# Sixteen more tokens taken out of the dense expert products and served by gathered rows, with GpSimd and ScalarE doing their arithmetic

## The reference

```python
q = (xf @ wq).reshape(t, PEER_HEADS, PEER_QDIM)
s1, s2 = q_first_half @ keys1.T, q_second_half @ keys2.T
v1, i1 = lax.top_k(s1, PEER_TOPK); v2, i2 = lax.top_k(s2, PEER_TOPK)
...                                   # the best 16 of the 16 x 16 sums of each head
expert = ...                          # (t, 128) numbers of experts
gate = jax.nn.softmax(top_s, axis=-1).reshape(t, -1)
z = jnp.einsum('cd,ced->ce', xc, u[ec])
act = jax.nn.gelu(z, approximate=False) * gc
out = jnp.einsum('ce,ced->cd', act, v[ec])
```

## Time and profile before

| | us |
|---|---|
| median of three runs | 3151.75 |
| lowest of them | 3145.31 |
| the profiled execution | 3146.41 |
| its span, first to last instruction | 3144.4 |
| TensorE busy | 3106.8 (99%) |
| VectorE busy | 2407.6 (77%) |
| ScalarE busy | 1743.9 (55%) |
| GpSimd busy | 308.2 (10%) |
| the eight PEER blocks, U0 to V3 | 1764.6 to 3130 of the span |

### The profile page before, as it was taken

How to read it: one execution, slowest core, us unless ns; L and a number is a source line. 1 busy time by engine, 2 the same in 40 slices (tenths; PEclk the granted TensorE clock), 3 DMA queues, 4 the chain that set the end, 5 groups by cost and what they waited for, 6 DMA issues and landing times.

```text
span 3144.4 us, 62060 instructions
## 1 busy us (share of the span) xinstructions
PE 3106.8 (99%) x24748; PEld 3003.6 (96%) x24748; DVE 2407.6 (77%) x3908; ACT 1743.9 (55%) x2400; POOL 308.2 (10%) x303
## 2 busy tenths in 40 slices
PE   9999999999999999999999999999999999999998
PEld 9999999999999999999999988999999999999997
DVE  8767777755556776666668999988799789988887
ACT  6444545777776655555655455554555545554454
POOL 2000000000000000000000022331133112210110
PEclk9999999999999999999999999999999999999999
DMA  5444435444444545555455555678867787665785
GB/s 203 147 160 148 169 115 211 161 169 163 160 164 171 185 168 182 176 180 177 164 188 180 185 199 202 245 264 287 297 236 251 274 287 249 244 214 188 259 291 194
DMA packets 117821, 637.37 MB, mean 203 GB/s; under 512 B 11633, under 2 KB 32497, under 8 KB 50417
## 3 DMA queue, kind: packets, MB, share of 16 engines
q1 hardware_dynamic: 98496, 565.49, 50.7%
q0 software_dynamic: 18864, 68.43, 6.7%
q10 hardware_dynamic: 288, 1.05, 0.1%
HBM read 632.57 MB, written 2.36 MB: 202 GB/s over the span
## 4 chain that ended last, share of the span: by engine, by line
PE 86%; DVE 8%; DVEq 2%; ACT 2%; DMA 1%; issue 1%; ACTq 0%; SPq 0%
PE bank L670 14%; PE bank L672 14%; PE bank L671 14%; PE bank L1153 11%; PE bank L1206 9%; PE bank L1154 5%; PE bank L1207 5%; DVE wl L1856 3%; PE bank L1196 2%; PE bank L1198 2%; PE bank L1197 2%; PE bank L1117 1%; PE bank L824 1%; PE bank L1156 1%; ACT wh L1344 1%
## 5 line engine op out<-in xcount | busy, mean ns | idle before, releaser
L1856 DVE TENSOR_TENSOR wl<-raw,wh 128x1024 fp32r<-128x1024 f32 x1052 | 1267.1, 1238 | 349.9 <-ACT wh L1344 341.1
L1344 ACT ACTIVATE wh<-raw 128x1024 fp32r<-128x1024 f32 x1052 | 1052.7, 1050 | 394.3 <-DMA raw<-w_in_a 128.6
L671 PE MATMUL bank<-hhl,wh 128*128 128x256 f32 x3568 | 989.1, 277 | 0.0
L670 PE MATMUL bank<-hhl,wh 128*128 128x256 f32 x3440 | 966.9, 281 | 1.0 <-DVE hhl L1904 1.0
L672 PE MATMUL bank<-hhl,wl 128*128 128x256 f32 x3440 | 953.4, 277 | 0.0
L671 PEld LDWEIGHTS bank<-hhl,wh 128*128 128x128 f32 x3568 | 673.4, 189 | 1.9 <-issue 1.7
L670 PEld LDWEIGHTS bank<-hhl,wh 128*128 128x128 f32 x3440 | 647.9, 188 | 5.1 <-issue 2.4
L672 PEld LDWEIGHTS bank<-hhl,wl 128*128 128x128 f32 x3440 | 647.2, 188 | 0.0
L1153 PE MATMUL bank<-hhl,wh 128*128 128x448 f32 x1920 | 625.0, 382 | 6.8 <-DVE wl L1856 6.7
L1154 PE MATMUL bank<-hhl,wl 128*128 128x224 f32 x2048 | 522.4, 265 | 0.0
L1206 PE MATMUL bank<-ahl,wh 128*128 128x448 f32 x1488 | 472.1, 374 | 2.4 <-DVE ahl L2570 2.1
(11 more groups left out here) (461 smaller groups left out, 4405.2 us busy)
## 6 DMA issues: line engine op xcount, KB each, us to landing
raw<-peer_u SPq DMA_DIRECT2D x128, 1024.0 KB
raw<-peer_v SPq DMA_DIRECT2D x128, 1024.0 KB
raw<-w_in_c SPq DMA_DIRECT2D x64, 1024.0 KB
raw<-w_in_a SPq DMA_DIRECT2D x63, 1024.0 KB
raw<-w_kv SPq DMA_DIRECT2D x32, 1024.0 KB
raw<-w_in_b SPq DMA_DIRECT2D x32, 1024.0 KB
raw<-w_out_a SPq DMA_DIRECT2D x16, 1024.0 KB
raw<-w_out_b SPq DMA_DIRECT2D x16, 1024.0 KB
```

Source lines behind the costliest of these rows:

```text
L670: eng.matmul(out, h_[:, k, :], high[:, k, :], start=(k == 0), stop=False)
L671: eng.matmul(out, h_[:, k, :], low[:, k, :], start=False, stop=False)
L1344: eng.activation(high_half(c, half), raw_half(c, half), ACT.Copy).then_inc(hi_ready, 1)
L1856: eng.tensor_tensor(low_half_out(c, half), raw_half(c, half), high_half(c, half).bitcast(F32), ALU.subtract).then_inc(lo_ready, 1)
```

## The change

48 of the 256 tokens are now outside the dense products, so `DENSE` is 208: the wide matmuls have 416 columns, the narrow ones and those of V2 have 208, and there are 26 gate turns. The 32 tokens of before keep their path; three of `ROW_TURNS` are rewritten for 26 gate turns, with as many steps in each block as before.

The 16 new tokens (`MORE`) are spread as 16 tokens x 8 groups, which makes 16 steps of each of the 4 kinds, 64 in all. Each has an indirect DMA of 0.5 MB (`fetch_more`) into one buffer, `rows_more`. `MORE_AT` gives them turns: 20 in V0, 21 in V1, 13 in V2, 10 in V3.

- Products with `u` (steps 0 to 31, in V0 and in turns 0 to 14 of V1): GpSimd waits for the landing, multiplies the row by the tokens into `more_scaled`, and issues the next fetch; ScalarE's turn waits for GpSimd and sums `more_scaled` with a copy that accumulates.
- Sums with `v` (steps 32 to 63): ScalarE's turn waits for the landing and scales the row by its activation; GpSimd adds it to `x_more` and fetches the next. In V2 ScalarE scales in place and GpSimd fetches after its addition; else the fetch comes before it.
- ScalarE's part (`weigh_more`) stands at the end of its turn, after `high_part`.
- SP gets 16 small DMAs ahead of the loads of U1 (keys and gates of the new rows) and 8 ahead of those of V0 (the tokens), VectorE a wait for the first of them, GpSimd 8 DMAs behind step 15.
- TensorE gets 8 small matmuls in each of the two `row_sums`, behind a wait for the last sum.
- Several small tiles move and share memory, and some semaphores of an earlier stage are merged; the order of that stage's work is as it was.

```diff
 LAST = P // GROUPS
-DENSE = T - LAST
+MORE = 16
+MORE_GROUPS = P // MORE
+ROWED = LAST + MORE
+DENSE = T - ROWED
 TURNS = DENSE // TG
 ROWS = SLOTS_PER_TOKEN // GROUPS
+MORE_ROWS = SLOTS_PER_TOKEN // MORE_GROUPS
+ALL_ROWS = ROWS + MORE_ROWS
 ROW_TURNS = {
-    "U1": [n for n in range(3, BJ) if n % 2 == 1 or n >= TURNS],
+    "U1": [n for n in range(5, BJ) if n % 2 == 1 or n >= TURNS],
     "V0": [n for n in range(BJ) if n % 4 != 3 and n != 20 or n == 23],
-    "U2": [n for n in range(BJ) if n % 2 == 1 or n >= TURNS - 2],
+    "U2": [n for n in range(BJ) if n % 2 == 1 or n >= TURNS],
     "V1": [0, 1, 2, 4] + [n for n in range(9, BJ) if n % 4 != 3],
-    "U3": [n for n in range(TURNS + 1) if n % 2 == 1 or n >= TURNS],
+    "U3": [n for n in range(TURNS + 2) if n % 2 == 1 or n >= TURNS],
     "V2": [20, 22, 24, 26, 28, 29, 30, 31],
     "V3": [n for n in range(27) if n % 8 != 7],
 }
@@ -70,6 +75,21 @@
 for _k, _v in ROW_TURNS.items():
     for _n in _v:
         ROW_AT[_k, _n] = len(ROW_AT)
+assert len(ROW_AT) == 4 * ROWS
+MORE_TURNS = {
+    "V0": [n for n in range(BJ) if n % 8 in (0, 2, 3, 5, 6)],
+    "V1": [n for n in range(16) if n % 4 != 3] + [n for n in range(20, 30) if n != 24],
+    "V2": [n for n in range(13) if n % 2 == 0] + [n for n in range(20, BJ) if n % 2 == 0],
+    "V3": [n for n in range(23) if n % 5 in (0, 2)],
+}
+MORE_AT = {}
+for _k, _v in MORE_TURNS.items():
+    for _n in _v:
+        MORE_AT[_k, _n] = len(MORE_AT)
+assert len(MORE_AT) == 4 * MORE_ROWS
+MORE_GELU_AT = 17
+MORE_GATED_AT = 17
+MORE_IN_PLACE = range(MORE_AT["V2", 0], MORE_AT["V3", 0])
...
+                if (name, b) == ("U", 1):
+                    eng.wait_ge(sQ["x_out"], 16)
+                    eng.wait_ge(sQ["slots_step"], 1)
+                    eng.sem_inc(sp_passed, 1)
+                    for q in range(MORE_GROUPS):
+                        slots = slice(q * MORE_ROWS, (q + 1) * MORE_ROWS)
+                        eng.dma_start(row_keys[q * MORE:(q + 1) * MORE, :, ROWS:ALL_ROWS],
+                                      place[P - ROWED:P - LAST, NT - 1, :, slots]).then_inc(sQ["keys_in"], 16)
+                        eng.dma_start(row_gate[q * MORE:(q + 1) * MORE, ROWS:ALL_ROWS],
+                                      tops[P - ROWED:P - LAST, NT - 1].rearrange("p h k -> p (h k)")[:, slots]).then_inc(sQ["keys_in"], 16)
+                if (name, b) == ("V", 0):
+                    eng.wait_ge(sQ["slots_step"], 4)
+                    for q in range(MORE_GROUPS):
+                        eng.dma_start(x_more[q * MORE:(q + 1) * MORE, :], x_rows[0:MORE, 0:D // 2]).then_inc(sQ["more_x_in"], 16)
                 block_of(name, peer_u if name == "U" else peer_v, b)
...
+            def fetch_more(g):
+
+                kind, r = g // MORE_ROWS, g % MORE_ROWS
+                eng.indirect_dma_start(out=rows_more[:, :], out_offset=None, in_=peer_u_rows if kind < 2 else v_rows,
+                                       in_offset=bass.IndirectOffsetOnAxis(ap=left[kind // 2][:, kind % 2, ROWS + r:ROWS + r + 1], axis=0)).then_inc(more_in, 16)
+
+            def more_dot(g):
+
+                kind, r = g // MORE_ROWS, g % MORE_ROWS
+                eng.wait_ge(more_in, 16 * (g + 1))
+                if g > 0:
+                    eng.wait_ge(sQ["more_by_scalar"], g)
+                if r == 0 and kind == 0:
+                    eng.wait_ge(sQ["more_x_in"], 16 * MORE_GROUPS)
+                if r == 0 and kind == 1:
+                    eng.wait_ge(sQ["x_out"], 16 + 16 * MORE_GROUPS)
+                eng.tensor_tensor(more_scaled[:, :], rows_more[:, :], x_more[:, :], ALU.mult)
+                eng.drain().then_inc(sQ["more_by_gpsimd"], 1)
+                if kind == 0 and r == MORE_ROWS - 1:
+                    for q in range(MORE_GROUPS):
+                        eng.dma_start(x_more[q * MORE:(q + 1) * MORE, :], x_rows[0:MORE, D // 2:D]).then_inc(sQ["x_out"], 16)
+                fetch_more(g + 1)
+
+            def more_gates():
+
+                eng.wait_ge(sQ["more_by_scalar"], 2 * MORE_ROWS)
+                eng.tensor_tensor(row_dot[:, 0, ROWS:ALL_ROWS], row_dot[:, 0, ROWS:ALL_ROWS], row_dot[:, 1, ROWS:ALL_ROWS],
+                                  ALU.add).then_inc(sQ["more_step"], 1)
+                eng.wait_ge(sQ["more_step"], 2)
+                eng.tensor_tensor(row_act[:, ROWS:ALL_ROWS], row_act[:, ROWS:ALL_ROWS], row_gate[:, ROWS:ALL_ROWS],
+                                  ALU.mult).then_inc(sQ["more_step"], 1)
+
+            def more_sum(g):
+
+                r = g % MORE_ROWS
+                in_place, ends = g in MORE_IN_PLACE, r == MORE_ROWS - 1
+                eng.wait_ge(sQ["more_by_scalar"], g + 1)
+                if not in_place and not ends:
+                    fetch_more(g + 1)
+                if r > 0:
+                    eng.tensor_tensor((rows_more if ends else x_more)[:, :], (rows_more if in_place else more_scaled)[:, :], x_more[:, :], ALU.add)
+                eng.drain().then_inc(sQ["more_step" if ends else "more_by_gpsimd"], 1)
+                if in_place and not ends:
+                    fetch_more(g + 1)
+
+            def take_more(g):
+
+                if g < 2 * MORE_ROWS:
+                    more_dot(g)
+                else:
+                    more_sum(g)
 
             for name, b in PEER_ORDER:
                 for n in range(BJ):
                     if name == "U":
                         add_dots(b, n)
+                    if (name, b, n) == ("V", 0, 0):
+                        eng.wait_ge(sQ["gated"], TURNS)
+                        fetch_more(0)
+                    if (name, b, n) == ("V", PAIRED, BJ // 2 + LOWER_ROWS_SUM_AT + 2):
+                        eng.wait_ge(sQ["row_sums_step"], 3)
+                        fetch_more(3 * MORE_ROWS)
+                    if (f"{name}{b}", n) in MORE_AT:
+                        take_more(MORE_AT[f"{name}{b}", n])
+                    if (name, b, n) == ("V", 1, MORE_GATED_AT):
+                        more_gates()
...
             def row_sums(f, bank):
 
                 eng.wait_ge(s["row_sums_step"], 3 * f + 1)
+                eng.wait_ge(s["more_step"], f + 4)
+                for c in range(FH):
+                    eng.matmul(B[bank][:, FH * LAST + c * MORE:FH * LAST + (c + 1) * MORE], rows_more[:, c * P:(c + 1) * P],
+                               token_more[:, :], start=True, stop=True)
...
+            def weigh_more(b, n):
+
+                if (f"V{b}", n) in MORE_AT:
+                    g = MORE_AT[f"V{b}", n]
+                    kind, r = g // MORE_ROWS, g % MORE_ROWS
+                    if kind < 2:
+                        eng.wait_ge(s["more_by_gpsimd"], g + 1)
+                        eng.activation(more_scaled[:, :], more_scaled[:, :], ACT.Copy,
+                                       accum_out=row_dot[:, kind, ROWS + r:ROWS + r + 1]).then_inc(s["more_by_scalar"], 1)
+                    else:
+                        eng.wait_ge(more_in, 16 * (g + 1))
+                        if kind == 2 and r == 0:
+                            eng.wait_ge(s["more_step"], 3)
+                        elif r > 1 and g not in MORE_IN_PLACE:
+                            eng.wait_ge(s["more_by_gpsimd"], g - (kind - 2))
+                        out_ = x_more if r == 0 else rows_more if g in MORE_IN_PLACE else more_scaled
+                        eng.activation(out_[:, :], rows_more[:, :], ACT.Copy, scale=row_act[:, ROWS + r:ROWS + r + 1]).then_inc(s["more_by_scalar"], 1)
...
+                    if b == 1 and n == MORE_GELU_AT:
+                        eng.wait_ge(s["more_step"], 1)
+                        eng.activation(row_act[:, ROWS:ALL_ROWS], row_dot[:, 0, ROWS:ALL_ROWS], ACT.Gelu).then_inc(s["more_step"], 1)
...
+                    weigh_more(b, n)
...
-                x_ = xT[:, f * FH:(f + 1) * FH, DENSE:T]
+                more_ = xT[:, f * FH:(f + 1) * FH, DENSE:DENSE + MORE]
+                eng.tensor_tensor(more_, B[bank][:, FH * LAST:FH * ROWED].rearrange("p (c t) -> p c t", t=MORE), more_, ALU.add)
+                x_ = xT[:, f * FH:(f + 1) * FH, DENSE + MORE:T]
                 eng.tensor_tensor(x_, B[bank][:, 0:FH * LAST].rearrange("p (c t) -> p c t", t=LAST), x_, ALU.add).then_inc(s["row_sums_step"], 1)
 
...
+            eng.wait_ge(s["keys_in"], 16 * 2 + 2 * 16 * MORE_GROUPS)
```

135 lines of the change are left out of this document (77 added, 58 removed).

## The result

The changed kernel takes 3300.4 us in the median, the kernel before 3150.9 us beside it. The ratio is 1.0477, with a 95% interval of 1.0446 to 1.0508: slower by 4.8%, 150 us. The prediction was 3190, with a range up to 3245. V0 and V1 lose, as forecast, but nearly twice as much: 56 and 62 us where 31 and 33 were forecast. V2 and V3, which were to gain 6 us, lose 41 together.

A forecast was written before the change was run, and what follows sets the result against it. TensorE's matmuls were taken to bound the PEER blocks. From 3146.4 us: -22 for six blocks, +31 for V0 and +33 for V1 by the new chain, +2 for the clock, giving 3190; range 3115 to 3245.

The forecast's parts named there:

- Narrower matmuls, 14 ns a pair, nothing in V2: TensorE's dense products: only the wide matmul shrinks, 14 ns a pair, 7 us a block, 50 us over seven blocks.
- U0 -1.5: Block U0: VectorE sets its middle, so only the last few units gain, 1.5 us.
- U1 -5.5: Block U1: gains 7 and 0.5 us, less 2 for a start behind 16 small DMAs, so 5.5 us.
- U2 and U3 -4.5 each: Blocks U2 and U3: VectorE stays just below the bound, at 97%, so each gains 4.5 us, with a late start.
- Landing 6.4, multiplication 3.1, between them 0.1: 9.6 us: Product step in V0 and V1: fetch landing, GpSimd's multiplication and handover in line, 9.6 us, against 7.8 and 6.5 asked.
- 0.1 us between them: Product step: handing over between landing, GpSimd's multiplication and next fetch takes only 0.1 us.
- slower chain: Rival: the chain decides, a product step takes 11.3 us, V2's steps fall behind too, 3262 us; chance 0.29.
- Sum steps 7.8 us, the addition hidden in the landing; V2's and V3's spaced steps can be followed: Sum steps: landing 6.4, scaling 1.1, handover 0.3, no addition; V3 gains 5.5 us, V2 0.5.
- VectorE becomes the bound: Rival in V0 and V1: GpSimd's operations slow VectorE, 1.8 us each, and the chain keeps up; 3116 us, chance 0.07.
- GpSimd below a third: Reading of the profile before: GpSimd is busy less than a third of the PEER blocks.
- The bytes: 0.5 MB more a step on V0's DMA share of 0.84, weighed only for the slower chain, no term in the sum.
- Clock +2: TensorE's lower clock after waits in V0 and V1: mostly covered while it waits for the chain, 2 us more.

The follow-up runs named there:

- e13: e12 with its 32 steps at the changed kernel's closer spacing; 3210.1 us.
- e12: e1 with 32 of the 64 new steps, set 3 to 4 turns apart, and the row fetch issued ahead of the step; 3160.9 us.
- e10: e1 with GpSimd issuing VectorE's row fetch ahead of the new step in each turn; 3257.1 us.
- e2: Changed kernel with only its narrower dense products, without the 64 new steps; 3120.0 us.
- e1: Changed kernel without drains: GpSimd's operation raises the semaphore itself, and GpSimd waits for it before overwriting the buffer; 3259.3 us.
- e5: e2 plus only GpSimd's 62 multiplications of 1024 columns, on a buffer nobody waits for; 3153.1 us.
- e6: e2 plus the 62 multiplications of 1024 columns done by VectorE, none by GpSimd; 3146.0 us.
- e11: e2 plus 64 plain transfers of 512 KB, started by ScalarE into buffers nobody reads; 3146.3 us.
- e3: Kernel before the change with a drain on GpSimd behind each of V3's 22 row fetches; 3165.6 us in one run, beside 3147.2.
- e4: e1 with GpSimd's multiplications and additions cut from 1024 columns to 16, gathers, scalings and waits kept; 3197.1 us.

## Why the prediction was wrong

**What the 150 us are.** From the runs: -27 for the narrower products; +30 GpSimd's operations against VectorE, +26 the bytes, +8 ScalarE's scalings, each alone; +39 the drains. That is 76. The other 74 us are what the steps cost together beyond these parts, found by subtraction, as if the parts added up. They are put down to steps asked for faster than they can follow and to row fetches queued with them. e13 less e12 shows the kind: 47 us for the same number of steps closer together. How the 74 split between the chain and the queue isn't settled: the two change places with the order, as e10 shows. What failed in the prediction is therefore the product step (the drain), the claim that V3's and V2's steps can be followed, and two costs put at nothing, GpSimd's hold on VectorE and the bytes.

**Step by step.**
- *Narrower matmuls, 14 ns a pair, nothing in V2.* Right. A pair in V0 of e2 takes 0.30 us, three matmuls of 208 columns in V2 of the changed kernel 0.34. The seven blocks were to bring 50 us; 22 of it was to show outside V0 and V1. e2 brings 27 in all, and in its profile 11 of it outside V0 and V1.

```profile
2179.69 0.36 PE L1301 MATMUL bank<-ahl,wh 128*128 128x416 f32 x1
2179.89 0.26 PE L1302 MATMUL bank<-ahl,wl 128*128 128x208 f32 x1
2179.99 0.37 PE L1301 MATMUL bank<-ahl,wh 128*128 128x416 f32 x1
```

```profile
2959.82 0.27 PE L1309 MATMUL bank<-ahl,wh 128*128 128x208 f32 x1
...
2960.16 0.27 PE L1309 MATMUL bank<-ahl,wh 128*128 128x208 f32 x1
```

- *U0 -1.5:* +0.6. *U1 -5.5:* -6.3. *U2 and U3 -4.5 each:* +2.5 and +3.5. They start with TensorE waiting for `gates_b` (11.2 us in 19 waits over both). VectorE's "97%" had no room; e2 too has 171.3 and 172.9 us there. The text named this as a sign of being wrong.
- *Landing 6.4, multiplication 3.1, between them 0.1: 9.6 us.* The landing was right: from issue to landing 5.8 us in the median of V0's 20 gathers in the changed kernel, and in e1 6.7 us on average from issue to multiplication where GpSimd waited for it. The multiplication takes 2.50 us on average, 2.35 where VectorE is out of the way. The 3.1 was drawn out from means that probably hold waits for VectorE: the additions of 224 columns with the mean of 0.97 us in the earlier trace rows take 0.67 us at the shortest. The estimate of 2.25 us from the figure of the Trainium skill (GPSIMD Engine Reference, Elementwise side-by-side cycle accounting) was nearer.

```profile
L699 POOL TENSOR_TENSOR more_scaled<-rows_more,x_more 128x1024 f32<-128x1024 f32 x32 | 79.9, 2496 | 95.6 <-DMA rows_more<-peer_u_rows,left 95.5
```

- *0.1 us between them.* **This step failed.** The drain stood in the diff, and the prediction gives no price of its own to it. It waits for a landing: V0's product steps are 11.0 us apart, 1.4 more than forecast. Without drains (e1) they are 9.7 apart, with the shorter multiplication making up for the longer gaps, and V0 takes 196.1 us for the 193.9 forecast. The "slower chain" had nearly the right step, 11.3 us, but from a landing of 7.9 and a multiplication of 3.3, which the runs don't show: that was luck. That its 3262 us are near the 3259 of e1 is luck too, for the steps of e1 are 9.7 us apart.
- *Sum steps 7.8 us, the addition hidden in the landing; V2's and V3's spaced steps can be followed.* **This failed too.** The additions of V1 are 9.3 us apart, 8.2 without the drains (e1). The addition is hidden from the step, but it, the waits before it and the drain stand in GpSimd's queue ahead of the row fetches, and the addition stops VectorE. V3 was to give 5.5 us and lost 33: 11 by the drain (e1), 12 by the order (e10); the other 10 aren't divided. V2 was to gain 0.5 us and lost 8. The prediction asked only whether a step fits in its turns and never what is queued behind it.
- *VectorE.* The rival "VectorE becomes the bound" had the price, 1.8 us for each operation of GpSimd (1.5 measured), and the forecast had it at zero, without a reason. VectorE had 32 idle us in V0, and the wait costs in spite of them, 30 us in all (e5): it falls also on `ahl` and on the weights that TensorE needs next. A mechanism that was priced in a rival belonged into the sum at some share. "GpSimd below a third" was read wrong, too: it is busy 62 of 171.6 us in U1 and 59 of 171.5 in U2.
- *The bytes* were looked at as a risk for the landing only. 26 us.
- *Clock +2.* Far too little. TensorE is busy 1368 us in the eight blocks, 1309 in e2 with the same products: 59 us more. Its waits grow from 34 to 156 us. The clock accounts for nearly all of the 59: in V0, V1 and V3 busy time times granted clock is within 1.5 us of that in e2 (V0: 156.3 and 154.9). So 122 us of waiting went with nearly half as much again in matmuls at the lower clock; both are in every price above. A wait may not be put at its own length.

Left open: how much of the 74 us is chain and how much queue. No complete version here beats the kernel before. If VectorE did the new operations itself, its part and the bytes alone, 24 and 26 us by e6 and e11, would be more than the 27 that e2 gives.

## What to carry to other kernels

Before work is moved to an engine that "has room", price what it does to its neighbours: an operation of GpSimd on two SBUF operands held VectorE's until it ended, and 2.08 us there cost the kernel no less than 1.22 on VectorE itself (30 and 24 us for 62 of them). On a queue that also issues gathers, let the operation raise its own semaphore and wait for that; a drain waits for the gathers. And ask of each in-order queue what stands behind the new wait: 32 steps of 8 to 10 us asked for each 5 to 8 us, most of them in V0, cost 47 us more than 32 asked for each 15 to 20.

## What was not expected of the hardware

- A drain in GpSimd's queue lasted until the gather issued ahead of it had landed, with GpSimd idle: the four fetches shown from e3 are 6.4 to 8.1 us apart, three of them 0.7 us behind the moment at which VectorE takes the row before. 22 drains cost 18 us.
- The wait for the shared port goes both ways: GpSimd's operations on 16 columns in e4 took 0.22 us when alone and up to 1.26 us when VectorE was in the middle of one of its own on two SBUF operands; that one ended 0.09 us behind VectorE's.
- After a wait of 6.4 us TensorE ran 6.0 us at a granted 0.50, its lower level of 1.2 GHz; the first matmul of 416 columns there took 0.72 us and those behind it 0.59, for 0.37 at 1.00.
